# A five-bank attention stage with early operands, and a ring of 16 page pairs for the cached values

## The chip, the cores and the metric

The kernel runs on one core of one Trainium2 chip. The metric is the device time of one execution in microseconds (us). Before the change the median of three runs is 3783.51 us (3782.46 to 3790.58).

## The reference, cut to what matters

The kernel computes one inference step of a decoder layer: input projection, attention beside a state-space branch, output projection, gated feed-forward. Only the attention stage is touched by the change. It has two halves. The prompt half is a strictly causal attention over 2048 positions with 8 heads of 64 channels; the sample half has 8 sequences of one new token each, and each attends to 8192 cached positions, which lie in 64 pages of 128 positions named by a page table.

```
def stick_breaking(q, k, v, bias, q_pos, k_pos):
    z = jnp.einsum('bqhd,bkhd->bhqk', q, k) * (HEAD_DIM ** -0.5)
    z = z + bias[None, :, None, None]
    mask = k_pos[None, :] < q_pos[:, None]
    log_keep = jnp.where(mask, jax.nn.log_sigmoid(-z), 0.0)
    later = lax.cumsum(log_keep, axis=3, reverse=True) - log_keep
    w = jnp.where(mask, jnp.exp(jax.nn.log_sigmoid(z) + later), 0.0)
    return jnp.einsum('bhqk,bkhd->bqhd', w, v)
...
k_past = cache_k[l][page_table].reshape(bs, n_past, N_ATT_HEADS, HEAD_DIM)
v_past = cache_v[l][page_table].reshape(bs, n_past, N_ATT_HEADS, HEAD_DIM)
```

## The kernel before, in words

All of it is in `stage_attention` (from L903). The work runs in eight rounds (`rounds`, L985). Round b works on head b of the prompt and, beside it, on sample sequence b. Round 0 is written out, rounds 1 to 7 are a hardware loop, and a few drain steps follow.

A round has 40 steps, one for each unit (c, j): the 512 queries of chunk c against the 128 keys of block j, chunk 3 first, j falling. A unit goes through a pipeline over the engines. TensorE (PE) writes the logits z by two products (L1373) into PSUM bank s % 4. ScalarE (ACT) makes ln(1 + exp z) in `X` (L1176, L1178). VectorE (DVE) makes the clamped softplus (L1264, one step later). GpSimd (POOL) masks a diagonal block (L1127) and keeps the running sum `S` of the keys already done (L1134, L1140). PE then adds the two triangular or all-ones sums to the same bank (L1383, L1386, L1391, two steps after the logits), ACT takes the exponential into `Wt` (L1184), and PE multiplies with the values (L1406, three steps after, two units at a time). Banks 4 and 5 hold the outputs, bank 6 (`Q_B`) the query of the sample, and bank 7 (`S_B`) the sample's sums.

The sample's work is laid into the same steps. In steps 0 to 31 DVE multiplies one pair of key pages with the query, which it reads from bank 6 (L1295), and reduces the product (L1300). In steps 32 to 37 the sample's softmax-like weights are made (L1309 to L1322 on DVE, L1200 to L1207 on ACT, L1414 and L1415 on PE). In the odd steps up to 31 of the next round PE multiplies two pairs of value pages with these weights (L1343). The last sequence has no next round: its 32 pairs come in a tail after round 7. Key and value pages lie in rings of 8 pairs each (`Kr`, `Vr`).

Before a head's first unit, q and k of the head are split in two parts that TensorE can take at full precision: ACT makes three copies and the bias row (L1163 to L1169), DVE two differences (L1255, L1256). This is done by chunk at steps 0, 1, 5 and 9 of the head's own round (`SPLIT_AT`, L983), from two slots of raw chunks. Each round begins with the spread of the sample's query on DVE (L1248) and its four transposes on PE (L1359); the bias of the head is copied at step 0 (L1269).

Every load is issued by the SyncE queue (SP), in one order, written out in `round_` from L1057. For each n of 0 to 31 it reads two page numbers into registers, waits until DVE has summed key pair n, and issues two DMAs for key pair n + 8 (L1042); then it reads two page numbers, waits until PE has used value pair n of the sequence before, and issues two DMAs for value pair n + 8. Between them lie the raw chunks of q and k (L1021, four DMAs a chunk, four chunks a round), the values of the head (L1030, four a round), and at the round's head three copies of page-table rows (L1060) with a wait for their landing (L1063). A wait in this order holds back all that stands behind it.

Of the kernel before, what the change touches and what calls it, by code (L numbers as in the profile page):

```python
# [15 lines left out]
F32 = mybir.dt.float32  # L16
F32R = mybir.dt.float32r
I32 = mybir.dt.int32
# [4 lines left out]
P = 128  # L23
# [867 lines left out]
KSLOTS, VSLOTS = 8, 8  # L891
# [13 lines left out]
def stage_attention(nc, A, keep):  # L905
# [17 lines left out]
    with ExitStack() as ctx:  # L923
        m = Stage(nc, ctx, "att")
        ident = keep["ident"]
        NX, NW = 4, 4
        row_last, row, row_next = (m.sb(n, [1, NPG], I32) for n in ("row_last", "row", "row_next"))
        table, table_in = m.sb("table", [1, NS, NPG], I32), m.sb("table_in", [1, NS, NPG], I32)
        qf, kf = m.sb("qf", [P, 2, CH]), m.sb("kf", [P, 2, CH])
# [18 lines left out]
        qsT = m.sb("qsT", [P, QT, NS])  # L948
        qrep = m.sb("qrep", [P, QT, P])
        z_s, x_s, w_s = (m.sb(n, [P, H, NPG]) for n in ("z_s", "x_s", "w_s"))  # L950
        R = m.sb("R", [P, H, NPG + 1])
# [4 lines left out]
        Q_B, S_B = 6, 7  # L956
# [6 lines left out]
        q_wide, q_rows = m.sem("q_wide"), m.sem("q_rows")  # L963
        qk_loaded, v_piece = m.sems("qk_loaded", 2), m.sems("v_piece", NCH)
# [14 lines left out]
        LAGS = 5  # L979
        K_END = NKK  # L980
        VG = 2 * PP
        QUAD = P // VG
        SPLIT_AT = {0: 3, 1: 2, 5: 1, 9: 0}  # L983

        def rounds(eng, body):  # L985

            body(0, range(NU), True, False)
# [14 lines left out]
        with nc.Block() as block:  # L1002

            @block.sync
            def _(sp):
                sp.dma_start(table_in[:], A["page_table"][:, :].rearrange("(o b) r -> o b r", o=1)).then_inc(table_loaded, 16)
                sp.dma_start(bias_all[:], A["sb_bias"].to_broadcast([P, H])).then_inc(loaded, 16)
                sp.dma_start(qsT[:], A["qT"].rearrange("(j p) n -> p j n", p=P)[:, :, T:NT]).then_inc(loaded, 16)
# [4 lines left out]
                def load_qk(b, c):  # L1013

                    i = NCH - 1 - c
                    if not (isinstance(b, int) and b == 0 and i < 2):
                        sp.wait_ge(qk_lo, b * 2 * NCH + 2 * (i - 1))
                        sp.nop().then_inc(waited, 1)
                    for x, src in ((qf, "qT"), (kf, "kT")):
                        for half in range(2):  # L1020
                            sp.dma_start(x[half * HD:(half + 1) * HD, i % 2, :], A[src][bass.ds(b * HD, HD), c * CH:(c + 1) * CH]  # L1021
                                         ).then_inc(qk_loaded[i % 2], 16)
# [27 lines left out]
                for c in (3, 2):  # L1050
                    load_qk(0, c)
# [5 lines left out]
                def round_(b, first, last):  # L1057
# [6 lines left out]
                    for n in range(NKK):  # L1064
# [35 lines left out]
            def _(pool):  # L1100
# [5 lines left out]
                pool.memset(R[:], 0.0).then_inc(consts, 1)  # L1106
                pool.wait_ge(consts, 6)
# [38 lines left out]
            def _(act):  # L1146
# [8 lines left out]
                def round_(b, steps, first, rest):  # L1155
                    for s in steps:
                        if s in SPLIT_AT and not rest:
                            c = SPLIT_AT[s]
                            i = NCH - 1 - c
                            cs = slice(c * CH, (c + 1) * CH)  # L1160
                            act.wait_ge(qk_loaded[i % 2], 64 * (b * (NCH // 2) + i // 2 + 1))
                            act.wait_ge(z_ready, b * NU)
                            act.activation(qhh[:, cs], qf[:, i % 2, :], ACT.Copy).then_inc(qk_hi, 1)  # L1163
# [1297 lines left out]
```

## Time and profile before

| what | us |
| --- | --- |
| median of the runs | 3783.51 |
| the profiled execution | 3787.69 |
| its span, first to last instruction | 3786.0 |
| attention, first logits to the store of the samples' output | 739.6 to 1878.2 |
| TensorE busy over the span | 3361.4 (89%) |
| VectorE busy | 2032.3 (54%) |
| ScalarE busy | 1405.9 (37%) |
| GpSimd busy | 640.7 (17%) |

The busy shares are of the whole span; the attention stage is about 30% of it. PE busy is time in which a matmul was under way, and PEclk is the granted clock of TensorE as a share of full speed, 2.4 GHz (0.50 is the lower level, 1.2 GHz). The DMA share is the mean busy share of the 16 DMA engines.

### The profile page before, as it was taken

Reading aid. Unit: us, or ns where it says so; the run is one execution under the profiler, and the core shown is the slowest. Engines: PE = TensorE matmul, PEld = TensorE weight load, DVE = VectorE, ACT = ScalarE, POOL = GpSimd, SP = SyncE. Lnnn points to the kernel's source line nnn. Section 1 sums busy time; section 2 is a strip of 40 time slices with the busy share of each in tenths; the row PEclk is TensorE's granted clock in tenths of the full one; section 3 lists DMA queues with packets and bytes.
Section 4 is the critical chain, followed back from the end, with each engine's and each line's share of the span. In section 5 each row is a group of like instructions: output and inputs, shape, how many; then the busy total and the mean of one; then the engine's idle time right before and its main releaser. Section 6 shows DMA issues by size and latency. Waiting matters only on the chain. (4 is left out here: it accounts for less than half of the span.)

```text
span 3786.0 us, 49489 instructions
## 1 busy us (share of the span) xinstructions
PE 3361.4 (89%) x14901; PEld 2310.0 (61%) x14901; DVE 2032.3 (54%) x2777; ACT 1405.9 (37%) x2206; POOL 640.7 (17%) x902
## 2 busy tenths in 40 slices
PE   4999864589898899889579979999999999999998
PEld 3888742333333333333268857778777877777777
DVE  5010139788788779779245545534553445345542
ACT  4110101256555555555233334423442344223332
POOL 1000047533333333333101100000000000000000
PEclk8999877799999999999789989999999999999999
DMA  4121251377797788779545543343334333433333
GB/s 122 62 72 46 77 77 25 97 238 220 258 310 252 250 280 272 254 259 302 195 139 150 150 115 90 98 146 100 95 103 136 106 95 101 138 121 119 123 113 113
DMA packets 487649, 569.70 MB, mean 150 GB/s; under 512 B 64808, under 2 KB 308616, under 8 KB 485321
## 3 DMA queue, kind: packets, MB, share of 16 engines
q1 hardware_dynamic: 482950, 549.81, 47.7%
q10 hardware_dynamic: 4328, 17.05, 1.2%
q8 instruction: 83, 1.36, 0.2%
q14 instruction: 112, 0.91, 0.1%
q0 software_dynamic: 176, 0.56, 0.0%
HBM read 506.91 MB, written 59.30 MB: 150 GB/s over the span
## 5 line engine op out<-in xcount | busy, mean ns | idle before, releaser
L2088 PE MATMUL ffn_bank<-ffn_xh,ffn_wh 128*128 128x512 f32 x1408 | 557.9, 396 | 18.7 <-DVE ffn_wl L2302 18.3
L2088 PE MATMUL ffn_bank<-ffn_xl,ffn_wh 128*128 128x512 f32 x1408 | 549.5, 390 | 0.0
L2088 PE MATMUL ffn_bank<-ffn_xh,ffn_wl 128*128 128x512 f32 x1408 | 549.0, 390 | 0.0
L1383 PE MATMUL att_bank<-att_X,att_negtri 128*128 128x512 f32 (+3 forms) x640 | 304.0, 557 | 65.1 <-POOL att_X L1127 53.0
L1140 POOL TENSOR_TENSOR att_S<-att_S,att_X 128x512 f32<-128x512 f32 (+3 forms) x256 | 277.7, 1085 | 332.9 <-PE att_bank L1391 183.7
L2088 PEld LDWEIGHTS ffn_bank<-ffn_xh,ffn_wh 128*128 128x128 f32 x1408 | 265.0, 188 | 94.7 <-DVE ffn_wl L2302 31.2
L1300 DVE TENSOR_REDUCE att_z_s<-att_prod 128x16 f32<-128x1024 f32 x256 | 313.0, 1223 | 8.8
L1295 DVE TENSOR_TENSOR att_prod<-att_Kr,att_bank 128x1024 f32<-128x1024 f32 x256 | 310.4, 1213 | 1.7 <-issue 1.7
L2088 PEld LDWEIGHTS ffn_bank<-ffn_xh,ffn_wl 128*128 128x128 f32 x1408 | 265.0, 188 | 56.3
L2088 PEld LDWEIGHTS ffn_bank<-ffn_xl,ffn_wh 128*128 128x128 f32 x1408 | 265.3, 188 | 52.5
L2306 DVE TENSOR_TENSOR ffn_wdl<-ffn_wdf,ffn_wdh 128x1024 fp32r<-128x1024 f32 x88 | 107.5, 1225 | 338.6 <-ACT ffn_wdh L2212 338.5
L1176 ACT ACTIVATE att_X<-att_bank 128x512 f32<-128x512 f32 (+2 forms) x320 | 170.5, 533 | 250.7 <-PE att_bank L1373 250.0
L1391 PE MATMUL att_bank<-att_S,att_negones 128*128 128x512 f32 (+3 forms) x576 | 260.2, 534 | 0.0
L2339 DVE TENSOR_SCALAR ffn_conv<-ffn_gbuf,ffn_prm 128x512 f32<-128x512 f32 x88 | 48.1, 546 | 387.1 <-issue 202.9
L1184 ACT ACTIVATE att_Wt<-att_bank 128x512 f32<-128x512 f32 (+2 forms) x320 | 169.7, 530 | 174.3 <-PE att_bank L1391 171.2
L2190 PE MATMUL ffn_bank<-ffn_wdh,ffn_hh 128*128 128x512 f32 x704 | 221.2, 396 | 11.8 <-DVE ffn_wdl L2306 9.7
L2302 DVE TENSOR_TENSOR ffn_wl<-ffn_stage,ffn_wh 128x1024 fp32r<-128x1024 f32 x176 | 215.0, 1222 | 30.9 <-ACT ffn_wh L2207 29.8
L2212 ACT ACTIVATE ffn_wdh<-ffn_wdf 128x1024 fp32r<-128x1024 f32 x88 | 92.8, 1059 | 349.5 <-PE ffn_bank L2190 320.0
L1264 DVE SCALAR_TENSOR_TENSOR att_X<-att_X,att_bank 128x512 f32<-128x512 f32 (+2 forms) x320 | 191.7, 600 | 54.1 <-ACT att_X L1178 53.2
L2190 PE MATMUL ffn_bank<-ffn_wdl,ffn_hh 128*128 128x512 f32 x704 | 219.5, 393 | 0.0
L2190 PE MATMUL ffn_bank<-ffn_wdh,ffn_hl 128*128 128x512 f32 x704 | 219.4, 393 | 0.0
L2207 ACT ACTIVATE ffn_wh<-ffn_stage 128x1024 fp32r<-128x1024 f32 x176 | 185.8, 1056 | 81.2 <-PE ffn_bank L2088 65.4
(377 smaller groups left out, 5792.4 us busy)
## 6 DMA issues: line engine op xcount, KB each, us to landing
att_Kr<-in_cache_k_dram SPq DMA_DIRECT2D x512, 256.0 KB, 3.7
att_Vr<-in_cache_v_dram SPq DMA_DIRECT2D x512, 256.0 KB, 3.8
ffn_wdf<-in_w_down_dram SPq DMA_DIRECT2D x108, 512.0 KB, 3.6
ffn_stage<-in_w_gate_dram SPq DMA_DIRECT2D x89, 512.0 KB, 3.9
ffn_stage<-in_w_up_dram SPq DMA_DIRECT2D x88, 512.0 KB, 4.6
qku_work<-in_x_prompt_dram SPq DMA_DIRECT2D x16, 512.0 KB
att_qf<-qT_dram SPq DMA_DIRECT2D x64, 128.0 KB, 3.5
att_kf<-kT_dram SPq DMA_DIRECT2D x64, 128.0 KB, 3.6
```

The source lines that it names most:

```text
L1140: pool.tensor_tensor(new[:, r:], old[:, r:], x[:, r:], ALU.add).then_inc(s_part, 1)
L1176: act.activation(x, bank[:, s % 4, cols(s):], ACT.Exp).then_inc(e_ready, 1)
L1184: act.activation(Wt[:, u % NW, cols(u):], bank[:, u % 4, cols(u):], ACT.Exp).then_inc(w_ready, 1)
L1264: stt(x, x, LN_TOP, z, ALU.min, ALU.max).then_inc(sp_ready, 1)
L1295: tt(pr, Kr[:, kk % KSLOTS], bank[:, Q_B, :][:, None, :].to_broadcast([P, PP, AW]), ALU.mult).then_inc(k_used, 1)
L1300: dve.tensor_reduce(z_s[:, :, kk * PP:(kk + 1) * PP].rearrange("p h r -> p r h"), prod[:, kk % 2, :].rearrange("p (k h d) -> p k h d", k=P ...
L1383: last = pe.matmul(bank[:, u % 4, o:], negtri[:], X[:, u % NX, o:], start=False, stop=True, skip_group_check=True)
L1391: last = pe.matmul(bank[:, u % 4, o2:], negones[:], S[:, (u - 1) % 2, o2:], start=False, stop=True, skip_group_check=True)
L2088: mm = pe.matmul(bank[:, first + f % 2, :], w[:, j, k, :], x[:, k, :], start=(k == 0 and n == 0), stop=(k == KD - 1 and n == 2))
L2190: mm = pe.matmul(bank[:, 2 * t + c, :], x[:, f, cols], w[:, sl, c * CH:(c + 1) * CH], start=(f == 0 and n == 0), stop=(f == FT - 1 and n = ...
L2207: act.activation(wh[:, j], wf[:, j], ACT.Copy).then_inc(w_hi[j], 1)
L2302: tt(wl[:, j], wf[:, j], wh[:, j].bitcast(F32), ALU.subtract).then_inc(w_lo[j], 1)
```

## The change: what it does

Five PSUM banks hold logits in place of four, so the second pass over a unit comes three steps after its logits in place of two (`LAG`), and the value product one step later as well. To free a bank, the sample's query is transposed into bank 7 at step 37 of the round before and copied to SBUF (`q_wide`); DVE's product reads it there. The copy takes one ACT instruction; the transposes and the spread move from the round's head into steps 37 and 36. The outputs move to banks 5 and 6.

The raw q and k get four chunk slots. Chunks 3, 2 and 1 of the next head are split at steps 33, 35 and 38 of the round before, chunk 0 at step 3 of its own; the bias is copied at step 28. SP issues all four chunks of head 0 before the first key pages, and later ones at n = 9, 11, 13, 15 of the round before. The head's value pieces 1 and 0 move to n = 1 and 5. The value product of the samples moves from odd to even steps, one step later. Round 7 is written out too.

The ring of value pages has 16 pairs in place of 8; the ring of key pages keeps 8. SP issues value pair n + 16 where it issued pair n + 8, and its count of instructions a round stays.

```diff
-KSLOTS, VSLOTS = 8, 8
+KSLOTS, VSLOTS = 8, 16
...
-        NX, NW = 4, 4
+        NX, NW, NZ = 4, 4, 5
-        qf, kf = m.sb("qf", [P, 2, CH]), m.sb("kf", [P, 2, CH])
+        qf, kf = m.sb("qf", [P, NCH, CH]), m.sb("kf", [P, NCH, CH])
...
+        q_wide = m.sb("q_wide", [P, AW])
-        Q_B, S_B = 6, 7
+        O_B, S_B = NZ, 7
...
-        LAGS = 5
+        LAG = 3
+        LAGS = LAG + 3
+        Q_AT = K_END + 5
-        SPLIT_AT = {0: 3, 1: 2, 5: 1, 9: 0}
+        SPLIT_NEXT = {NKK + 1: 3, NKK + 3: 2, LAST[1] + 3: 1}
+        BIAS_AT = LAST[3] + 13
...
-            with eng.Fori(1, H) as b:
-                body(b, range(NU), False, False)
-            body(H, range(LAGS), False, True)
+            with eng.Fori(1, H - 1) as b:
+                body(b, range(NU), False, False, False)
+            body(H - 1, range(NU), False, True, False)
+            body(H, range(LAGS), False, False, True)
+        def splits(b, s, first, last):
+            now = [(b, 1)] if first and s == 1 else [(b, 0)] if s == 3 else []
+            return now + ([(b + 1, SPLIT_NEXT[s])] if s in SPLIT_NEXT and not last else [])
...
-                    if not (isinstance(b, int) and b == 0 and i < 2):
-                        sp.wait_ge(qk_lo, b * 2 * NCH + 2 * (i - 1))
+                    if not (isinstance(b, int) and b == 0):
+                        sp.wait_ge(qk_lo, (b - 1) * 2 * NCH + 2 * (i + 1))
...
-                for c in (3, 2):
+                for c in reversed(range(NCH)):
                     load_qk(0, c)
...
-                        if n < 2:
-                            load_qk(b, 1 - n)
-                        if n == 2 and not first:
-                            load_v_head(b, 0)
-                        if not last and n in (14, 15):
-                            load_qk(b + 1, 3 if n == 14 else 2)
-                        if not last and n in (20, 30):
+                        if not first and n in (1, 5):
+                            load_v_head(b, 1 if n == 1 else 0)
+                        if not last and n in (9, 11, 13, 15):
+                            load_qk(b + 1, 3 - (n - 9) // 2)
+                        if not last and n in (20, 31):
                             load_v_head(b + 1, 3 if n == 20 else 2)
-                    if not last:
-                        load_v_head(b + 1, 1)
...
+                def copy_queries(b):
+                    act.wait_ge(q_turned, b + 1)
+                    act.wait_ge(k_used, b * NKK)
+                    act.activation(q_wide[:], bank[:, S_B, :], ACT.Copy).then_inc(q_copied, 1)
...
+                        if s == Q_AT + 1 and not last and not rest:
+                            copy_queries(b + 1)
...
-                            tt(pr, Kr[:, kk % KSLOTS], bank[:, Q_B, :][:, None, :].to_broadcast([P, PP, AW]), ALU.mult
+                            tt(pr, Kr[:, kk % KSLOTS], q_wide[:, None, :].to_broadcast([P, PP, AW]), ALU.mult
...
+                        if s == Q_AT - 1 and not last:
+                            spread_queries(b + 1)
...
-                            if not first or s >= 4:
-                                pe.wait_ge(w_ready, units_to(b, s, 4, first))
+                            if not first or s >= NZ:
+                                pe.wait_ge(w_ready, units_to(b, s, NZ, first))
...
-                        r, u = behind(b, s, 2, first, rest)
+                        r, u = behind(b, s, LAG, first, rest)
...
-                        r, u = behind(b, s, 3, first, rest)
+                        r, u = behind(b, s, LAG + 1, first, rest)
...
-                        if s < NKK and not first:
-                            samples_v(b - 1, s)
+                        if 1 <= s <= NKK and not first:
+                            samples_v(b - 1, s - 1)
                         if s == K_END + 1 and not first:
                             finish_sequence(b - 1)
+                        if s == Q_AT and not last_head:
+                            turn_queries(b + 1)
```

## Rows read from the trace of the kernel before

**Rows 1.** Round 2, busy us of PE, PEld, DVE, ACT, POOL; PEclk, DMA share, GB/s:

```profile
1003.80:1139.90 136.10, 123.77 (x488) 52.05 (x488) 111.42 (x134) 77.64 (x143) 48.82 (x63) 0.97 0.84 270
```

**Rows 2.** Waits of PE in round 2 (total us, times, longest):

```profile
PE att_bank L1383 <- POOL att_X L1127: 5.8, 5, 1.9
PE att_bank L1373 <- ACT att_qlb L1169: 3.8, 1, 3.8
PE att_bank L1359 <- DVE att_qrep L1248: 2.6, 1, 2.6
```

**Rows 3.** PE in order of time (start, duration): round starts, a full step, the tail:

```profile
739.62 0.45 PE L1373 MATMUL att_bank<-att_qhh,att_khl 128*128 128x128 f32 x1 [3.05 <-issue]
...
872.59 0.47 PE L1373 MATMUL att_bank<-att_qhh,att_khl 128*128 128x128 f32 x1 [1.90 <-ACT att_qlb L1169]
...
957.02 0.50 PE L1373 MATMUL att_bank<-att_qhh,att_khl 128*128 128x512 f32 x1
...
960.39 0.51 PE L1373 MATMUL att_bank<-att_qhh,att_khl 128*128 128x512 f32 x1
...
1694.93 0.47 PE L1373 MATMUL att_bank<-att_qhh,att_khl 128*128 128x128 f32 x1 [4.00 <-ACT att_qlb L1169]
...
1831.06 1.50 PE L1343 MATMUL att_bank<-att_Vr,att_w_s 128*8 128x512 f32 x12
```

**Rows 4.** Waits of the SP queue in round 2:

```profile
SPq L1042 <- PE att_bank L1343: 3.9, 1, 3.9
SPq L1042 <- DVE att_z_s L1300: 3.2, 1, 3.2
SPq L1028 <- PE att_bank L1406: 2.7, 1, 2.7
SPq L1063 <- DMA att_row_next<-att_table: 1.0, 1, 1.0
```

**Rows 5.** The SP queue in order of time, inside round 1:

```profile
931.87 0.85 SPq L1042 DMA_DIRECT2D att_Kr<-in_cache_k_dram  x2
933.47 0.85 SPq L1042 DMA_DIRECT2D att_Vr<-in_cache_v_dram  x2
934.68 1.16 SPq L1021 DMA_DIRECT2D att_qf<-qT_dram  x2
...
937.88 0.86 SPq L1042 DMA_DIRECT2D att_Kr<-in_cache_k_dram  x2
```

**Rows 6.** DVE in order of time, round 0, one step to the next:

```profile
821.79 1.21 DVE L1295 TENSOR_TENSOR att_prod<-att_Kr,att_bank 128x1024 f32<-128x1024 f32 x1
...
824.77 1.21 DVE L1295 TENSOR_TENSOR att_prod<-att_Kr,att_bank 128x1024 f32<-128x1024 f32 x1
```

**Rows 7.** The SP queue at the start of the stage:

```profile
730.69 1.17 SPq L1021 DMA_DIRECT2D att_qf<-qT_dram  x2
...
736.89 7.46 SPq L1042 DMA_DIRECT2D att_Kr<-in_cache_k_dram  x10
```

**Rows 8.** DVE in round 0, the split of chunk 1:

```profile
763.95 0.68 DVE L1255 TENSOR_TENSOR att_qlb<-att_qf,att_qhh 64x512 fp32r<-64x512 f32 x1 [8.49 <-ACT att_kh L1165]
```

**Rows 9.** What the DMA engines moved in the tail, 1840 to 1870 us:

```profile
DMA packets 5347, 9.76 MB, mean 325 GB/s; under 512 B 593, under 2 KB 593, under 8 KB 5345
```

**Rows 10.** DVE in round 2, step 32, an operation with two SBUF inputs:

```profile
1118.19 0.69 DVE L1309 TENSOR_TENSOR att_z_s<-att_z_s,att_bias_all 128x512 f32<-128x512 f32 x1
```

**Rows 11.** POOL, the mask of a diagonal block, twice in round 2:

```profile
1118.35 0.84 POOL L1127 TENSOR_TENSOR att_X<-att_X,att_keepm 128x128 f32<-128x128 f32 x1 [3.82 <-DVE att_X L1264]
...
1130.79 0.45 POOL L1127 TENSOR_TENSOR att_X<-att_X,att_keepm 128x128 f32<-128x128 f32 x1 [1.52 <-DVE att_X L1264]
```

**Rows 12.** The page: POOL's running sum over the whole kernel (busy us, mean ns):

```profile
L1140 POOL TENSOR_TENSOR att_S<-att_S,att_X 128x512 f32<-128x512 f32 (+3 forms) x256 | 277.7, 1085 | 332.9 <-PE att_bank L1391 183.7
```

**Rows 13.** ACT in round 3, the split of a chunk, first and last instruction:

```profile
1161.87 0.63 ACT L1163 ACTIVATE att_qhh<-att_qf 128x512 fp32r<-128x512 f32 x1 [0.40 <-issue]
...
1163.56 0.72 ACT L1169 ACTIVATE att_qlb<-att_wide,att_bias_now 64x512 fp32r<-64x512 f32 x1
```

More of the change, by code:

```diff
@@ new lines, in copy_queries, with round_ @@
+                def copy_queries(b):
+                    act.wait_ge(q_turned, b + 1)
+                    act.wait_ge(k_used, b * NKK)
+                    act.activation(q_wide[:], bank[:, S_B, :], ACT.Copy).then_inc(q_copied, 1)
+                for c in (3, 2):
+                    split(0, c)
+                copy_queries(0)
+                def round_(b, steps, first, last, rest):
+                    for s in steps:
+                        if not rest:
+                            for at in splits(b, s, first, last):
+                                split(*at)
@@ L1183, in round_ @@
                                 act.wait_ge(av_done, units_to(r, u, NW, first))
-                            act.activation(Wt[:, u % NW, cols(u):], bank[:, u % 4, cols(u):], ACT.Exp).then_inc(w_ready, 1)
-                        r, u = behind(b, s, 4, first, rest)
+                            act.activation(Wt[:, u % NW, cols(u):], bank[:, u % NZ, cols(u):], ACT.Exp).then_inc(w_ready, 1)
+                        r, u = behind(b, s, LAG + 2, first, rest)
                         if u is not None and U[u][1] == 0:
@@ L1190, in round_ @@
                             act.wait_ge(o_copied, r * NCH + chunks - 1)
-                            act.activation(o_odd[:], bank[HD:P, 4 + c % 2, :], ACT.Copy).then_inc(odd_copied, 1)
-                        r, u = behind(b, s, 5, first, rest)
+                            act.activation(o_odd[:], bank[HD:P, O_B + c % 2, :], ACT.Copy).then_inc(odd_copied, 1)
+                        r, u = behind(b, s, LAG + 3, first, rest)
                         if u is not None and U[u][1] == 0:
@@ L1261, in softplus @@
                                 return
[L1262 removed]
+                            x, z = X[:, u % NX, cols(u):], bank[:, u % NZ, cols(u):]
                             dve.wait_ge(l_ready, r * NU + u + 1)
                             stt(x, x, LN_TOP, z, ALU.min, ALU.max).then_inc(sp_ready, 1)
[L1266 to L1269 removed]
+                        if s == BIAS_AT and not rest and not last:
+                            set_bias(b + 1)
                         if s == 0 or not rest:
                             softplus()
[L1272 removed]
+                        r, u = behind(b, s, LAG + 2, first, rest)
                         if u is not None and U[u][1] == 0:
@@ L1337, in samples_v @@
                         pe.wait_ge(w_s_ready, b + 1)
+                        pe.wait_ge(q_copied, min(b + 2, NS) if isinstance(b, int) else b + 2)
                     for i in (n - 1, n):
@@ L1352, in finish_sequence, with turn_queries, round_ @@
                     last.then_inc(col_ready, 1)
-                def round_(b, steps, first, rest):
-                    if not rest:
-                        pe.wait_ge(q_wide, b + 1)
-                        pe.wait_ge(k_used, b * NKK)
-                        for j in range(QT):
-                            last = pe.transpose(bank[:, Q_B, j * P:(j + 1) * P], qrep[:, j, :], ident[:])
-                        last.then_inc(q_rows, 1)
+                def turn_queries(b):
+                    pe.wait_ge(q_spread, b + 1)
+                    pe.wait_ge(logw_s, b)
+                    for j in range(QT):
+                        last = pe.transpose(bank[:, S_B, j * P:(j + 1) * P], qrep[:, j, :], ident[:])
+                    last.then_inc(q_turned, 1)
+                turn_queries(0)
+                def round_(b, steps, first, last_head, rest):
                     for s in steps:
```

103 lines of the change are left out of this document (54 added, 49 removed).

## The prediction

> **What bounds the kernel now.** I read the busy table by stretches first, then PE's waits, then the queue of SP. From the first logits to the store of the samples' output attention lasts 739.6 to 1878.2 us, 1139 of 3786. The eight rounds start 133.0 us apart (round 0) and (1694.93 - 872.59) / 6 = 137.1 us apart on average (rounds 1 to 6); round 7 takes 136.1 and then comes a tail of 47.1 [rows 3]. In round 2 PE is busy 123.8 of 136.1 us, DVE 111.4, ACT 77.6, POOL 48.8 [rows 1]. PE's 12.3 idle us have two places: 6.4 at the round's head (2.6 for the query's spread, 3.8 for the chunk's split and bias), and 5.8 before the second pass over diagonal blocks, which waits for POOL's mask [rows 2]. Everywhere else PE goes without a gap, a full step in 960.39 - 957.02 = 3.37 us [rows 3]. So PE's own work sets the round, and the twelve idle us are what this change can take.
>
> The second thing to see is who stands right behind PE. SP waits in a round only 3.9 + 3.2 + 2.7 us for other engines [rows 4], so its own work is 136.1 - 9.8 = 126.3 us a round (the 1.0 us for the table rows stays with it). Its beat shows the same: a pair of pages every 1.60 us whatever it loads, and 937.88 - 933.47 - 1.60 = 2.8 us more for a chunk of q and k [rows 5]. 64 pairs make 102.4 us, four chunks 11.2, value pieces and table rows the rest. DVE's own beat is 2.98 us a step while keys are multiplied [rows 6], 95.4 us for 32 steps.
>
> **Part 1: the round's head, rounds 1 to 7.** Gone from PE's path are 2.6 + 3.8 us of waits [rows 2]; the four transposes stay, now in step 37. The work is the same number of instructions: the ACT copy of the query is new, one of 0.6 us (the size of the split's own copies [rows 13]), beside PE. A split occupies ACT from 1161.87 to 1164.28, 2.4 us [rows 13], and three of four now fall in steps 33 to 38. I cost this at nothing, since the third step of lag covers it; if that cover is gone it is at most 2.4 us for each of three splits, 7 us a round, and I count 3 us of it as a rival.
>
> **Part 2: the lag of three.** The five waits of 5.8 us on POOL's mask [rows 2] have a longest of 1.9 us; a step is 3.37. One more step of distance covers each. PE's floor is then 136.1 - 12.2 = 123.9 us, a little less (I say 122), since after the idle head PE works some us at the lower clock (PEclk 0.97 over the round [rows 1]).
>
> **Part 3: what is late next.** SP's 126.3 us. The change leaves its instructions in number as they are, and moves a few past one another. Its waits for DVE's first sum and PE's first value pair fall away when it is late itself, and the wait at the round's end for a value piece is moved behind work long done. The key ring keeps 8 pairs, so a late SP reaches DVE some steps later, DVE's product waits in DVE's queue ahead of the softplus, and PE waits for that. The lead of the ring (8 steps of 3 us) holds for a round or so, then the round is SP's. I take 126.3 us a round for rounds 1 to 6: 6 x 126.3 = 757.8 against 822.3, a gain of 64.5. Both ends: 122 (PE's floor) gives 90; DVE's floor is 95.4 for the keys and about 24 for the last eight steps, 120, no bound. Round 7 issues 8 key pairs fewer, so PE's floor holds, 123.9 and 1 more for the longer drain: a gain of 11.2.
>
> The Trainium skill (DMA: Bandwidth & Descriptors, "Issuing engines are not separate DMA queues") says that the sequencer's time to start a DMA is usually small beside the DMA itself. Here the row speaks against it: 1.60 us of queue time for 0.52 MB, and the same bytes take 1.61 us at the tail's 325 GB/s [rows 5, 9]. By the rule SP would bound nothing and rounds would be 122; by the row they are 126.3.
>
> **Part 4: round 0.** It is DVE's: a beat of 2.98 us [rows 6]. Gone are 8.5 us in which DVE waits for the split of chunk 1, whose raw chunk was queued behind key pages [rows 8]. Added: SP issues four chunks before the first key page in place of two; two took 736.89 - 730.69 = 6.2 us [rows 7], so all key products start 6.2 later. The head of round 1 loses 1.9 us of wait in the row at 872.59 [rows 3] and the spread's, 2.5 as in round 2 [rows 2], together 4.4, and PE's logits run one DVE step further ahead of the softplus, 3.0. Against that I set 3 us for the port (part 6). Sum: 8.5 - 6.2 + 4.4 + 3.0 - 3 = 6.7, a gain; bounds 0 and 13.
>
> **Part 5: the ring of 16.** In rounds 1 to 7 nothing waits for value pages (no such row among PE's waits [rows 2]), so the ring brings nothing there, and it costs no instruction. In the tail, 24 pairs are loaded after 1831 us at 325 GB/s [rows 9], 1.61 us a pair, and PE waits for them. With 16 pairs already there 16 remain: a gain of 8 x 1.61 = 12.9. The 4.2 MB move to round 0, whose DVE does not wait for them; if it did, the gain would be gone, so 0 to 13.
>
> **Part 6: the product's operand.** DVE's key product now has both inputs in SBUF. Its own duration I leave at 1.21 us [rows 6]: half as many elements with two SBUF inputs took 0.69 [rows 10], twice that is 1.38, so up to 0.17 a step more, which fits into DVE's spare time. But POOL shows something: the mask that started inside that operation took 0.84 us, the same mask 12 us later 0.45 [rows 10, 11]. So such a DVE operation holds POOL up, by 0.39 us in that row. The reverse, DVE held by POOL, no row shows; it lies between 0 and the longest sum of POOL, 1.28 us (277.7 / 256 gives a mean of 1.09 over all shapes [rows 12]). I take 0.1 us a step, near zero, because DVE has 0.4 us to spare in a full step of PE (3.37 - 2.98), and where DVE is late POOL's sum starts from PE's product, beside DVE's reduction; that is the 3 us of round 0.
>
> The Trainium skill (SBUF — State Buffer, "Who interferes with whom") says that a DVE instruction with two SBUF inputs contends with a GpSimd instruction that reads SBUF, and that whichever starts first makes the other wait until its end. The trace agrees for one direction (0.84 beside 0.45 us). By the rule in full it is the slower rival below.
>
> **The sum.** 64.5 + 11.2 + 6.7 + 12.9 = 95.3. The profiled execution took 3787.7 (span 3786.0), so 3692.4; it lies 4.2 above the median of the runs, 3783.5, so 3688.
>
> **The rivals.**
> - PE stays the bound: rounds of 122. For it: SP's lateness has 8 pairs of lead, and the loads could slide. Against: a lead is spent once, 126.3 comes each round. Six rounds give 26 more, round 7 two: 3660.
> - ACT or DVE is late at the round's end, where three splits, the sample's exponentials and the query's copy now meet: rounds of 129 to 130. For: these eight steps hold 7.2 us of splits that were elsewhere. Against: ACT is busy 77.6 of 136 us [rows 1]. 7 x 3 = 21: 3709.
> - Slower: DVE's product waits for POOL's running sum. It decides from the point where a DVE step with keys exceeds 3.5 us, a wait of 0.52 us a step: then the keys take 112 us and, with 24 for the rest, the round is the old 136. At a wait of half a sum, 0.64 us, the step is 3.62, the round 140, 3 above the old mean: 7 x 3 = 21 slower, round 0 32 x 0.54 = 17 less its 6.7, the tail 12.9 back: 3783.5 + 18 = 3802. At 1.28 us it is near 3960. For: the 0.39 us above. Against: POOL is busy 48.8 of 136 us [rows 1], and a DVE that waits shifts until the two alternate.
> - No change (within 0.2%): some new wait gives all back; I see no such row.
>
> **How the numbers follow.** Forecast 0.50, PE the bound 0.20, crowded end 0.15, slower by the port 0.08, no change 0.03; 0.04 are for things not listed, half on each side. A measurement of this kernel can tell 0.2%, 8 us, from no change. Faster 0.87, same 0.03, slower 0.10. The range runs from 3655, just past PE's floor, to 3730, past the crowded end and a port that costs 6 us a round.
>
> **What would show it.** Right: PE's waits at L1359 and for the bias row gone; no wait for POOL's mask above 0.5 us; starts of rounds 126 us apart from round 2 on; SP's queue without a wait of over 1 us but for table rows; DVE's L1295 waiting for DMA of `att_Kr` late in the key steps; the tail 34 us. Wrong: rounds of 122 with SP waiting for DVE each round (the queue was no bound); L1295 much over 1.21 us, or idle before it released by POOL (the port); PE idle in steps 33 to 39.

## The result: 3731.2 us, and the profile after

| | before | after |
| --- | --- | --- |
| median of four runs each, same chip | 3785.32 (3782.46 to 3790.58) | 3731.23 (3729.65 to 3737.59) |
| ratio | | 0.9859, 95% interval 0.9842 to 0.9876 |
| span of the profiled execution | 3786.0 | 3729.7 |
| round 0 | 133.0 | 125.65 |
| rounds 1 to 6, mean | 137.1 | 132.9 |
| round 7 | 136.1 | 131.3 |
| tail | 47.1 | 34.4 |

The change gains 54 us of the 95 forecast; the forecast was 3688, with a range to 3730, and the median lies 1.2 us beyond it. Of the span's 56.3 us attention accounts for 7.3 + 25.2 + 4.8 + 12.7 = 50.0 by its four stretches (forecast 6.7, 64.5, 11.2, 12.9). The other 6.3 lie before the first logits (1.1) and behind the samples' store (1907.8 before, 1902.6 after). The change has nothing there, and this latter stretch came out between 1901.1 and 1907.6 in the experiments' profiles with no order to it: it is scatter. So the miss is one of rounds 1 to 7: 39.3 us in rounds 1 to 6 and 6.4 in round 7.

PE in order of time in the changed kernel, the starts of rounds 0, 1 and 7 and of the tail, against [rows 3]; then the samples' store on SP's queue:

```profile
738.56 0.48 PE L1415 MATMUL att_bank<-att_qhh,att_khl 128*128 128x128 f32 x1 [1.82 <-DVE att_khl L1283]
...
864.21 0.33 PE L1415 MATMUL att_bank<-att_qhh,att_khl 128*128 128x128 f32 x1
...
1661.37 0.33 PE L1415 MATMUL att_bank<-att_qhh,att_khl 128*128 128x128 f32 x1
...
1792.68 0.63 PE L1382 MATMUL att_bank<-att_Vr,att_w_s 128*8 128x512 f32 x4
```

```profile
1827.11 0.40 SPq L1101 DMA_DIRECT2D attT_dram<-att_att_s  x1
```

A round of the loop in the changed kernel by engines (columns as in [rows 1]), then what PE waited for in it, against [rows 2], and what SP's queue waited for, against [rows 4]:

```profile
1128.75:1262.03 133.28, 124.74 (x490) 54.07 (x488) 114.88 (x133) 77.61 (x145) 62.89 (x65) 0.96 0.86 276
```

```profile
PE att_bank L1390 <- DVE att_own L1261: 3.9, 1, 3.9
PE att_bank L1448 <- ACT att_Wt L1205: 3.2, 2, 2.7
PE att_bank L1425 <- POOL att_X L1135: 1.5, 1, 1.5
```

```profile
SPq L1053 <- DVE att_z_s L1336: 7.4, 1, 7.4
SPq L1074 <- DMA att_row_next<-att_table: 1.0, 1, 1.0
SPq L1053 <- PE att_bank L1382: 0.2, 1, 0.2
```

The waits aimed at are gone: the spread's 2.6 and the bias's 3.8 altogether, POOL's mask from 5.8 to 1.5. Two are new. PE waits 3.9 us at L1390 for DVE's product `att_own` of the finished sequence, and 3.2 us at the round's head for ACT's `Wt`, 2.7 of them in one stop. SP's own work is 133.3 - 7.4 = 125.9 us, as sized (126.3). But it waits for DVE's first key sum of the round, and that comes when the round before has ended: the queue does not bind, it is held to the round's beat.

Both new waits, seen close. DVE in order of time at steps 32 to 34:

```profile
1235.45 0.95 DVE L1345 TENSOR_TENSOR att_z_s<-att_z_s,att_bias_all 128x512 f32<-128x512 f32 x1
1236.44 0.57 DVE L1348 TENSOR_SCALAR att_x_s<-att_z_s 128x512 f32<-128x512 f32 x1
1236.93 1.47 DVE L1282 TENSOR_TENSOR att_qlb<-att_qf,att_qhh 64x512 fp32r<-64x512 f32 x1
1238.44 0.69 DVE L1283 TENSOR_TENSOR att_khl<-att_kf,att_khl 64x512 fp32r<-64x512 f32 x1
1239.16 0.69 DVE L1302 SCALAR_TENSOR_TENSOR att_X<-att_X,att_bank 128x512 f32<-128x512 f32 x1
1239.76 0.69 DVE L1261 TENSOR_TENSOR att_own<-att_bank,att_heads 128x512 f32<-128x512 f32 x1
```

and PE over the same time and at the head of the next round:

```profile
1235.98 0.65 PE L1448 MATMUL att_bank<-att_Wt,att_vh 128*64 128x128 f32 x4
1240.51 1.87 PE L1390 MATMUL att_bank<-att_one,att_own 128*128 128x1 f32 x8 [3.88 <-DVE att_own L1261]
1242.23 0.77 PE L1415 MATMUL att_bank<-att_qhh,att_khl 128*128 128x512 f32 x1
...
1267.37 1.09 PE L1448 MATMUL att_bank<-att_Wt,att_vh 128*64 128x128 f32 x4 [2.43 <-ACT att_Wt L1205]
```

DVE is never idle here. The split of chunk 3 (L1282, L1283) and a softplus stand ahead of the product in its in-order queue, and PE is ready from 1236.6. The stall then costs a second time. Busy time by stretches of 5 us around it:

```profile
1235.00:1240.00 5.00, 1.63 (x10) 0.71 (x8) 4.90 (x7) 4.55 (x9) 2.50 (x3) 1.00 0.98 318
1240.00:1245.00 5.00, 4.50 (x13) 3.27 (x14) 3.37 (x12) 1.23 (x2) 0.00 (x0) 0.51 1.01 353
1245.00:1250.00 5.00, 5.00 (x15) 2.33 (x13) 0.90 (x2) 3.06 (x6) 1.90 (x2) 0.80 0.97 329
```

After 3.9 idle us the granted clock is 0.51, the 1.2 GHz level, for five us, then 0.80 on the way back to 2.4. Against full speed these ten us lose 5 x 0.49 + 5 x 0.20 = 3.4 us of work, an estimate from the two rows, beside the 3.9. ACT at the head of the next round:

```profile
1262.52 0.26 ACT L1205 ACTIVATE att_Wt<-att_bank 128x128 f32<-128x128 f32 x1
1264.85 0.28 ACT L1197 ACTIVATE att_X<-att_bank 128x128 f32<-128x128 f32 x1 [2.07 <-POOL att_S L1148]
1265.16 0.31 ACT L1199 ACTIVATE att_X<-att_X 128x128 f32<-128x128 f32 x1
1266.84 0.38 ACT L1205 ACTIVATE att_Wt<-att_bank 128x256 f32<-128x256 f32 x1 [1.37 <-issue]
```

ACT is idle for 2.07 and 1.37 us, the second time with nothing that the profile shows to wait for. At the head of round 7, which is written out, these gaps are absent, and so they are at the head of round 1, the loop's first pass; PE's wait for `Wt` is 0.5 us in round 1 and 0.7 in round 7. So the loop's turn was suspected.

### The profile page after: what moved, and what is told of

It is laid out like the page before. It is cut to its first block and busy times, and to the rows that moved or that the text cites. A ratio compares the mean times of both kernels' runs of the same rounds, so it can differ in the third digit from the quotient of the medians.

```text
span 3729.7 us, 49239 instructions
## 1 busy us (share of the span) xinstructions
PE 3346.6 (90%) x14901; PEld 2314.4 (62%) x14901; DVE 2056.5 (55%) x2777; ACT 1408.0 (38%) x2214; POOL 759.2 (20%) x903
## 5 line engine op out<-in xcount | busy, mean ns | idle before, releaser
L1148 POOL TENSOR_TENSOR att_S<-att_S,att_X 128x512 f32<-128x512 f32 (+3 forms) x256 | 307.3, 1200 | 342.1 <-PE att_bank L1433 320.0
L1331 DVE TENSOR_TENSOR att_prod<-att_Kr,att_q_wide 128x1024 f32<-128x1024 f32 x256 | 334.0, 1305 | 5.4 <-issue 4.3
```

Source lines behind the costliest of these rows:

```text
L1148: pool.tensor_tensor(new[:, r:], old[:, r:], x[:, r:], ALU.add).then_inc(s_part, 1)
L1331: tt(pr, Kr[:, kk % KSLOTS], q_wide[:, None, :].to_broadcast([P, PP, AW]), ALU.mult).then_inc(k_used, 1)
```

## The experiments

Each is the changed kernel with the edit shown, unless it says otherwise; "round" is the mean of rounds 1 to 6, from PE's starts in the trace. None leaves out any of the work.

| kernel | median us | ratio to before, 95% | round us |
| --- | --- | --- | --- |
| changed kernel | 3731.23 | 0.9859 (0.9842 to 0.9876) | 132.9 |
| e2, own product first | 3710.43 | 0.9801 (0.9778 to 0.9824) | 129.2 |
| e3, split early | 3720.63 | 0.9830 (0.9807 to 0.9852) | 129.9 |
| e5, both | 3709.04 | 0.9790 (0.9769 to 0.9812) | 129.1 |
| e7, before + query in SBUF | 3836.71 | 1.0142 (1.0114 to 1.0169) | 144.0 |
| e1, value ring of 8 | 3748.08 | 0.9892 (0.9869 to 0.9915) | 132.9 |
| e6, before + ring of 16 | 3777.69 | 0.9971 (0.9950 to 0.9992) | 137.4 |
| e9, four banks, query in SBUF | 3762.70 | 0.9921 (0.9898 to 0.9943) | 136.1 |
| e10, four banks, query in PSUM | 3736.16 | 0.9854 (0.9838 to 0.9871) | 134.6 |
| e11, e2 + ring of five X | 3708.31 | 0.9776 (0.9740 to 0.9811) | 128.8 |
| e12, e10 + e2 | 3719.81 | 0.9799 (0.9762 to 0.9837) | 130.5 |
| e13, e2 + merged q/k loads | 3942.73 | 1.0388 (1.0350 to 1.0426) | 159 |
| e14, e11 + merged q/k loads | 3938.96 | 1.0381 (1.0342 to 1.0419) | as e13 |
| e15, e2 + ACT's rounds written out | 3691.92 | 0.9741 (0.9725 to 0.9757) | 127.5 |
| e16, e15 + k chunks issued by ACT | 3685.69 | 0.9724 (0.9707 to 0.9740) | 124.95 |
| e17, e16 + e3 | 3687.28 | 0.9734 (0.9716 to 0.9751) | 125.3 |
| e18, e12 + ACT's rounds written out | 3719.06 | 0.9813 (0.9795 to 0.9830) | 129.5 |

The kernel before was timed anew beside each group of experiments, on three chips, and its median lay between 3785.2 and 3795.7 us. So medians are compared within a group (e2, e3, e5, e7; e1, e6, e9, e10; e11 to e14; e15 to e18), and across groups the ratio is the safer figure: 0.001 of it is 3.8 us. The rounds come from one execution each; that of e10 was 10.7 us above its median and that of e15 5.6, so their rounds read long.

**The order at step 33 (e2, e3, e5).** e2 puts the finished sequence's product ahead of the split on DVE; e3 splits chunk 3 nine steps earlier; e5 has both.

```diff
+                        if s == K_END + 1 and not first and not rest:
+                            finish_sequence(b - 1)
                         if not rest:
                             for at in splits(b, s, first, last):
                                 split(*at)
...
-                        if s == K_END + 1 and not first:
-                            finish_sequence(b - 1)
```

```diff
-        SPLIT_NEXT = {NKK + 1: 3, NKK + 3: 2, LAST[1] + 3: 1}
-        BIAS_AT = LAST[3] + 13
+        SPLIT_NEXT = {LAST[3] + 9: 3, NKK + 3: 2, LAST[1] + 3: 1}
+        BIAS_AT = LAST[3] + 5
```

> The changed kernel with one order changed on VectorE: at step 33 the product for the finished sequence (L1261) stands ahead of the split of the next head's chunk 3, not behind it. Theory A (the end of the round is crowded on in-order queues: PE waits 3.8 to 4.0 us a round for that product, and works on at the low clock after it): the split's 1.47 + 0.69 us and the softplus's 0.6 leave the way of the product, the wait falls to about 1 us, with it some 3 us of slow work if the clock no longer falls: rounds of 133.2 become 127 to 130, the time about 3731 - 7 x 4 = 3703 (3690 to 3715). Theory B (contention of DVE and POOL for SBUF reads sets the round): no change, 3725 to 3735. Theory C (the page queue sets the round, 125.8 us of its own work): no round below 126, so nothing under about 3680; a gain down to there is possible.

> The changed kernel with the next head's chunk 3 split at step 24 in place of 33 (its old operands have been read by step 15), and the bias copied at step 20. Theory A: ACT loses 2.4 us and DVE 2.2 us ahead of the product PE waits for, the wait falls from 3.9 to about 1.5 us, rounds to 128 to 130: 3700 (3690 to 3715). DVE has 0.4 us to spare in a step with full width, so the split at step 24 costs nothing there. Theory B: no change or slower, since two more DVE operations with two SBUF inputs (64x512) run beside POOL: 3725 to 3745. Theory C: no round below 126.

> Both edits together: product ahead, chunk 3 split at step 24. Theory A: the wait for the product is nearly gone (below 0.5 us), but the second wait, 2.4 to 2.7 us for ACT's weights at the next round's first steps, stays: rounds of 126 to 129, 3690 (3675 to 3705), a little under the better of the two alone. Theory C: rounds reach 126 and SP's queue stops waiting for DVE's first sum (now 6 to 7.5 us a round). Theory B: as the changed kernel, 3731.

PE's waits in a round of e2:

```profile
PE att_bank L1448 <- ACT att_Wt L1205: 2.9, 2, 2.4
PE att_bank L1425 <- POOL att_X L1135: 1.5, 1, 1.5
PE att_bank L1456 <- DVE att_R L1354: 0.9, 1, 0.9
PE att_bank L1390 <- DVE att_own L1261: 0.7, 1, 0.7
```

The same round as above by engines, in e2:

```profile
1118.46:1246.18 127.72, 121.69 (x490) 51.93 (x488) 115.13 (x133) 77.21 (x145) 63.02 (x65) 0.99 0.88 285
```

An edit of order alone gives 21 us (22 by the ratios) and takes 3.2 of the 3.9 us of wait; PEclk of that round is 0.99, where it was 0.96. The round is 5.6 us shorter: 3.05 us is less busy PE for the same products (124.74 to 121.69), which is the clock's part, and 2.6 us is less waiting, since 0.9 us for DVE's `att_R` is new. The mean gain is smaller, 3.7 us a round, because PE's wait for `Wt` is 3.5 to 4.5 us in e2's rounds 4 to 6 (2.9 to 3.2 in the changed kernel) and its round 6 took 132.8 at PEclk 0.95. e3 leaves 2.2 of the wait and gives half; both together (e5) give no more than e2 and miss the 3690 expected. The stall at step 33 is shown, and its price with the clock. The wait for `Wt` stays in all three, and SP still waits 1.7 us for DVE in this round of e2.

**The port (e7, e9, e10).** e7 is the kernel before with the query's bank copied to SBUF by ACT, so that the product's operand changes, and one ACT copy a round is new:

```diff
+                                act.activation(q_sb[:], bank[:, Q_B, :], ACT.Copy).then_inc(q_copied, 1)
...
-                            tt(pr, Kr[:, kk % KSLOTS], bank[:, Q_B, :][:, None, :].to_broadcast([P, PP, AW]), ALU.mult
+                            tt(pr, Kr[:, kk % KSLOTS], q_sb[:, None, :].to_broadcast([P, PP, AW]), ALU.mult
```

e9 takes the fifth bank and the third step out of the changed kernel; e10 does so and leaves the query in bank 6:

```diff
-        NX, NW, NZ = 4, 4, 5
+        NX, NW, NZ = 4, 4, 4
-        LAG = 3
+        LAG = 2
```

> The kernel before with one thing of the change: ACT copies the sample's query from bank 6 to SBUF once a round (0.6 us, while it waits for the bias), and DVE's key product reads it there, so it has two SBUF inputs. Theory B (port): POOL's masks of diagonal blocks start behind that product and take 1.2 us more; with a lag of two steps PE waits for them, 14 of 16 a round: its wait of 5.8 us grows to 12 or more, rounds by 6 to 15 us, 3785 becomes 3830 to 3890. Theory A (the port costs little): 3785 to 3800.

> The changed kernel with four logit banks and a lag of two steps (the fifth bank and the third step undone), all else as changed: early operands, query in SBUF. Theory: the third step is what covers the port (POOL's masks of 1.0 to 1.5 us behind DVE's products). Without it PE waits for masks again, more than the 5.8 us a round of before, and its clock falls: rounds of 137 to 142, 3760 to 3800. Rival: the third step brought only the 5.8 us of before: rounds of 136, 3750.

> As the one with four banks and a lag of two, and the sample's query turned into bank 6, which is free again, and read there by DVE's product, so no operation more has two SBUF inputs. Only the early operands and the ring of the change are left. Theory: rounds lose the 6.4 us of the head and keep the 5.8 us for masks, and get the wait for the finished sequence's product (about 4 us and slow work behind it): 132 to 135, 3725 to 3750, within some us of the changed kernel; and well under the one with the query in SBUF, by 7 x 4 us or more. Rival (the port costs nothing at this place): both alike.

POOL's groups (busy us, mean ns, idle before) in a 144 us stretch of e7, sum and mask; then the same two in round 2 of the kernel before:

```profile
L1141 POOL TENSOR_TENSOR att_S<-att_S,att_X 128x512 f32<-128x512 f32 (+3 forms) x33 | 39.4, 1193 | 41.0 <-PE att_bank L1395 36.3 <-DVE att_X L1268 4.7
L1128 POOL TENSOR_TENSOR att_X<-att_X,att_keepm 128x128 f32<-128x128 f32 x16 | 16.0, 1000 | 32.8 <-DVE att_X L1268 32.8
```

```profile
L1140 POOL TENSOR_TENSOR att_S<-att_S,att_X 128x512 f32<-128x512 f32 (+3 forms) x32 | 34.7, 1086 | 40.3 <-PE att_bank L1391 23.2 <-DVE att_X L1264 17.1
L1127 POOL TENSOR_TENSOR att_X<-att_X,att_keepm 128x128 f32<-128x128 f32 x17 | 8.2, 480 | 41.1 <-DVE att_X L1264 41.1
```

A round of e7 by engines, against [rows 1]:

```profile
1308.67:1452.15 143.48, 128.70 (x488) 55.19 (x489) 114.73 (x134) 78.16 (x144) 60.99 (x64) 0.93 0.80 257
```

In the kernel before, that operand costs 51 us: the mask doubles to 1.0 us in the mean, and the round grows by 7. PE's waits for the mask account for 2.6 of these (5.8 to 8.4); the larger part is that PE is busy 4.9 us longer with the same products, at a PEclk of 0.93 where it was 0.97. The copy itself is not what costs: PE's waits at the round's head, for the spread and the bias, are 2.5 and 3.9 us, as before. The third step covers the slower masks in the changed kernel, where they take 1.08 us in the mean and mostly 1.4 beside DVE's products, while PE waits once for 1.5. With both taken out (e10) the time is that of the changed kernel, 0.9854 against 0.9859: the five-bank form, as built, brought nothing beyond what it cost. The port is one of these costs; the last experiment below shows another. With the port cost and without the cover (e9) it is 27 us slower than e10.

**The ring (e1, e6).** One line, `KSLOTS, VSLOTS = 8, 8` in the changed kernel and `8, 16` in the kernel before.

> The changed kernel with 8 pairs of value pages in the ring, as before. If the ring is worth what the tail shows (47.1 us before, 34 after), this is 13 us slower than the changed kernel, 3744, and its rounds are the same 133. If the ring also hides late pages in the rounds, the rounds lengthen and PE shows waits for pages.

> The kernel before with the ring of 16 value pairs alone. Same theory: the tail falls from 47 to 34 us, the rounds stay, 3785 - 13 = 3772. Rival: the 8 more pairs loaded in round 0 delay its key pages, and the gain is smaller.

Rounds are equal with and without. By the ratios to before, e1 gives (0.9892 - 0.9859) x 3785 = 12 us and e6 11 us (3 to 19 by its interval). The traces say it more sharply, and place it in the tail: 47.1 us in e1 against 34.4 in the changed kernel, and 34.4 in e6 against 47.1 before, 12.7 us both times (forecast 12.9).

**What the head of the round waits for (e11, e12, e15).** Two causes were open: the ring of four `X` buffers, or the turn of ACT's hardware loop. e11 adds a fifth `X` to e2 (the room comes from placing `bias_left` in `z_s`):

```diff
-        NX, NW, NZ = 4, 4, 5
+        NX, NW, NZ = 5, 4, 5
```

e15 writes ACT's rounds out and leaves all other engines in the loop:

```diff
-                rounds(act, round_)
+                round_(0, range(NU), True, False, False)
+                for b in range(1, H):
+                    round_(b, range(NU), False, b == H - 1, False)
+                round_(H, range(LAGS), False, False, True)
```

> The changed kernel with the finished sequence's product ahead of the split, and a ring of five softplus tiles X in place of four (a small bias tile shares the place of another, to fit). With the product ahead PE still waits 2.9 to 4.1 us a round at the next head's first steps for ACT's weights, and ACT waits there 4 to 6 us for POOL's sums before it may write X again. Theory A (ring of X is the cause): both waits fall below 1 us, rounds of 128 to 129 become 125.5 to 127, 3710 becomes 3690 (3680 to 3700). Rival: the wait moves to POOL's sums themselves, no change. Theory C (page queue, 126 us of own work) holds rounds at 126 whatever else is freed.

> Four banks, lag of two, query read from bank 6, early operands, ring of 16, and the finished sequence's product ahead of the split. If that order costs the same here as in the changed kernel (21 us), 3736 becomes 3715; the fifth bank with its lag is then worth the same few us with and without it. If the wait there is hidden behind POOL's masks (lag of two), the gain is smaller, 3725.

> The kernel with the product ahead of the split, and ACT's rounds 1 to 6 written out in place of a loop (the other engines keep theirs). At the head of a looped round ACT stands 3.2 + 1.5 us without work of its own, at the head of round 7, which is written out, not at all, and PE waits 2.9 to 4.1 us a round for ACT's weights there, 0.7 in round 7. Theory A2 (ACT's turn of the loop is the second wait): PE's wait falls to 0.7, rounds of 128 to 129 become 125 to 126, 3710 becomes 3693 (3685 to 3700). If it is the place in the pipeline and not the turn: no change. Theory C: SP's waits for DVE's first sum (1.7 to 3 us) go to zero and rounds stop at 126.

ACT at the same point of the same round in e11, then in e15:

```profile
1250.53 0.28 ACT L1198 ACTIVATE att_X<-att_bank 128x128 f32<-128x128 f32 x1 [3.52 <-issue]
1250.84 0.31 ACT L1200 ACTIVATE att_X<-att_X 128x128 f32<-128x128 f32 x1
1252.51 0.38 ACT L1206 ACTIVATE att_Wt<-att_bank 128x256 f32<-128x256 f32 x1 [1.35 <-issue]
```

```profile
1246.01 0.27 ACT L1197 ACTIVATE att_X<-att_bank 128x128 f32<-128x128 f32 x1
1246.31 0.31 ACT L1199 ACTIVATE att_X<-att_X 128x128 f32<-128x128 f32 x1
1246.78 0.38 ACT L1205 ACTIVATE att_Wt<-att_bank 128x256 f32<-128x256 f32 x1 [0.16 <-PE att_bank L1436]
```

A fifth `X` changes little but the label of the gap, which is now "issue": rounds of 128.8 against 129.2, and PE's wait for `Wt` in this round 4.3 us against 4.1 in e2. The theory of the ring fell. Written out, both gaps are gone, PE's wait for `Wt` is 0.5 us, and the time falls by another 18 us to 3691.9 (23 by the ratios), where the forecast had 3688. SP's waits in a round of e15, the only line that is left:

```profile
SPq L1074 <- DMA att_row_next<-att_table: 1.5, 1, 1.5
```

From round 2 on SP no longer waits for any engine, and DVE's product waits for pages (0.6 us in this round). Rounds 3 to 5 take 125.8 to 126.3 us; the mean of 127.5 has rounds 2 and 6 in it, 130.1 and 129.4, in which PE waited 3.4 us for `att_own`; what delayed it there is open. The rounds of 126 are the state which Part 3 of the prediction described.

**Is the queue then the bound (e13, e14, e16, e17)?** Two ways to take work from it. e13 and e14 load both halves of a q or k chunk by one DMA with a broadcast source; e16 lets ACT's queue issue the raw k chunks at steps 9 to 15.

```diff
-                        for half in range(2):
-                            sp.dma_start(x[half * HD:(half + 1) * HD, i, :], A[src][bass.ds(b * HD, HD), c * CH:(c + 1) * CH]
-                                         ).then_inc(qk_loaded[i], 16)
+                        sp.dma_start(x[:, i, :], A[src][bass.ds(b * HD, HD), c * CH:(c + 1) * CH][None].to_broadcast([2, HD, CH])
+                                     ).then_inc(qk_loaded[i], 16)
```

```diff
+                        if s in (9, 11, 13, 15) and not last and not rest:
...
+                            for half in range(2):
+                                act.dma_start(kf[half * HD:(half + 1) * HD, i, :], A["kT"][(b + 1) * HD:(b + 2) * HD, c * CH:(c + 1) * CH]
+                                              ).then_inc(qk_loaded[i], 16)
```

> As the one with the product ahead of the split (3710), and the raw q and k chunks loaded by two DMAs a chunk in place of four (one DMA fills both halves of the partitions): 8 DMAs fewer a round, about 5 of SP's 126 us. Theory C: SP waits only 1.7 to 3 us a round for DVE there, so the queue is nearly the bound: its lateness goes, rounds lose 1 to 3 us, 3700. Theory A alone: SP waits 5 us longer, the rounds stay, 3705 to 3713.

> Product ahead, ring of five X, merged loads. Theory C: where the ring of five alone stops at rounds of 126, this one goes on to 123 to 125, 3675 to 3685, at least 7 us under it. If SP bounds nothing, it equals the ring of five alone within noise.

> As the one with ACT written out, and the raw k chunks of the next head issued by ACT at steps 9 to 15, so SP's queue has 8 DMAs a round less, some 5 of its 126 us. Theory C: if rounds of ACT written out are held by the queue, these are 2 to 4 us shorter, about 123, 3675. If the queue holds nothing: the same, 3693, with SP waiting 5 us longer a round.

> As the last, and chunk 3 split at step 24. The product that PE waits for was then 0.8 us later than without the early split (1.5 beside 0.7), since DVE had less to do but later; so within 5 us of the last, either side. It is the version with every stall found so far taken out.

The SP queue of e13 in order of time, then DVE's longest waits over one round of it:

```profile
1452.31 0.60 SPq L1031 DMA_DIRECT2D att_qf<-qT_dram  x1
1453.03 5.49 SPq L1031 DMA_DIRECT2D att_kf<-kT_dram  x1
1459.78 3.91 SPq L1052 DMA_DIRECT2D att_Kr<-in_cache_k_dram  x1
```

```profile
DVE att_prod L1332 <- DMA att_Kr<-in_cache_k_dram: 30.8, 3, 11.8
```

What the DMA engines did while that queue was held, in e13 (the last two columns are their mean busy share and GB/s):

```profile
1453.10:1454.50 1.40, 1.40 (x10) 0.16 (x9) 1.37 (x2) 0.52 (x1) 0.32 (x1) 1.00 1.07 294
1456.00:1458.50 2.50, 2.50 (x10) 0.86 (x9) 2.46 (x4) 0.92 (x2) 0.43 (x1) 1.00 0.13 50
```

The merged loads failed at what they were for. Once the pages ahead of them have landed, the mean busy share of the 16 DMA engines is 0.13, what two of them fully busy would give, at 50 GB/s; it stays at 0.13 to 0.18 until 1464.5, and 0.5 MB at 50 GB/s is 10 us. In that time the second merged load of the pair, or the key DMA behind it, holds the queue for 2.8 to 5.5 us, where a merged load takes 0.6 when it is not held; in the round from 1238.7 us the second load was held in three of four pairs, for 4.5 to 5.5 us. So one DMA with a doubled source is no cheap form of two. By that e13 became a test of the opposite sign: a queue that is late costs the whole kernel, by the path queue, DVE's product, softplus, PE (159 us a round).

e16 takes the eight DMAs from SP in a way that works, but for less than expected (3675): 3685.7 us, 6.2 below e15, with no run of one inside the range of the other. Its rounds are 124.4 to 125.3, under the queue's 126. In round 3 of it SP waits for DVE again (3.7 us) and PEclk is 1.00 with four us of waits of PE, so PE is the bound. The bytes a round are those of e15, and they move at 294 to 296 GB/s where e15 had 290: it was the queue and not the DMA engines that held e15, a rival worth naming, because SP's beat of 1.60 us a pair is also what 325 GB/s gives. e17 adds nothing to e16. The changed kernel is 45.5 us above e16 by the medians, 51 by the ratios.

**The fifth bank, with and without ACT's turn (e12, e18).** e12 is e10 with the product ahead of the split, and e18 is e12 with ACT's rounds written out, that is, e15 with the four banks of e10.

> Four banks, lag of two, query in PSUM, product ahead, ACT written out: what the fifth bank is worth once the two waits at the round's end are gone. With the fifth bank the time is expected at 3693; here PE still waits some 4 to 6 us a round for masks: rounds of 130, 3715. If it lies within 5 us of the five-bank form, the fifth bank only pays for the port contention it brings.

PE's waits in a round of e12, then in one of e18:

```profile
PE att_bank L1420 <- POOL att_X L1135: 8.7, 6, 2.4
PE att_bank L1443 <- ACT att_Wt L1203: 0.6, 1, 0.6
```

```profile
PE att_bank L1423 <- POOL att_X L1135: 8.2, 5, 2.4
```

In the four-bank form the masks hold PE, and the turn costs next to nothing. ACT stands for 2.02 + 1.40 us at the round's head in e12 too, but PE waits 0.5 to 1.3 us for `Wt` in its rounds 2 to 6, not 2.9 to 4.5, and writing ACT's rounds out changes the time by 0.7 us (3719.8 to 3719.1; the ratios 0.9799 and 0.9813 do not tell them apart). With five banks and three steps the same edit gives 18. So the turn is a cost that the form with five banks brings into view, beside that of the port. While the turn stays, the form is worth little (0.9801 in e2, 0.9799 in e12); once it is gone, 3719.1 - 3691.9 = 27 us. Why three steps of lag expose the turn and two do not was not tried.

## Why the prediction was wrong

- **Part 1, the failing step.** "... three of four now fall in steps 33 to 38. I cost this at nothing, since the third step of lag covers it". The lag covers the way from logits to softplus. It does not cover an instruction for which PE waits in the same step: the finished sequence's product, behind the split on DVE. That is 3.9 us of wait a round and about 3 us of work at the low clock, and e2 takes back 21 us. The rival of a crowded end named the place (129 to 130 a round); it was the right mechanism, priced at 3 us a round where e2 gives 3.7 in the mean, and it missed the second stall beside it.
- **Not in the prediction at all:** ACT's loop turn, 3.4 us of idle ACT and 2.9 to 3.2 of PE's in rounds 2 to 6. e15 takes back 18 us. It is not the removal of the waits for the spread and the bias that let it appear: e9, e10 and e12 have them removed too, with a lag of two, and PE waits there for `Wt` at most 1.3 us a round. It came with the five banks and the third step. Writing out the loop of the kernel before was not tried.
- **Part 3, the size right and the role wrong.** SP's own work is 125.9 us (forecast 126.3). It binds only when both stalls are out (e15: 125.8 to 126.3 in rounds 3 to 5, 127.5 in the mean). Of the 39.3 us missing in rounds 1 to 6 (6 x 6.6), e2 and e15 return 6 x 5.4 = 32. For round 7 the forecast took PE's floor from round 2, 123.9 us and 1 for the drain. But PE is busy 127.2 us in round 7 (128.2 before), and waits 4.2 more, 1.6 of them for `att_own`. So it gained 4.8 where 11.2 were forecast.
- **Part 2.** Right: PE's waits for the mask went from 5.8 to 1.5, although the port made the masks longer, 0.48 to 1.08 us in the mean. That the third step would have to cover masks of 1.4 us was not foreseen; e9 and e10 show that it did.
- **Part 4.** Forecast 6.7, measured 7.3, in part by luck. DVE's wait of 8.5 us for chunk 1 is gone, as forecast, and the first key product comes 5.06 us later (745.50 against 740.44; forecast 6.2). But DVE's beat is unchanged at 2.99, so the 3 us set for the port do not show. The two terms for the next round's head, 7.4 together, must then have come to about 3.9 (7.3 - 8.5 + 5.1); which of them was too large is open. (For the spread the sum has 2.5 us where [rows 2] have 2.6.)
- **Part 5.** Forecast 12.9, measured 12.7, and again 12.7 in the tails of e1 and e6.
- **Part 6.** DVE's product takes 1305 ns in the mean, 0.09 a step more (forecast 0.1). The price lay on POOL's side, whose busy time in a round rose from 48.8 to 62.9 us, and was hidden. The forecast had no term for that, and e7 shows the 51 us which it costs when uncovered, most of it by the clock. The slower rival had named the wrong victim: not DVE behind the sum, but PE behind the mask.
- **The range** ended at 3730 because the rivals were taken one at a time. A crowded end (3709) with a second, unnamed stall of about its size is what happened, and that lies at the range's edge.

## What to carry to other kernels

When waits are cleared from the bound engine's path, list for every step that receives moved work each instruction on the same in-order queue that another engine awaits in that same step; lag hides only the chain which it lengthens. A deeper pipeline can expose a wait that the shallow one hid (here a loop's turn on ACT), so test an edit in both forms before calling it worthless. Price a stall of some us on TensorE twice, for the idle time and for the low clock after it; here that was 3.2 and 3.05 us in one round. An engine's own work is a bound only after every stall that is longer than its slack is gone.

## What the hardware showed that was not expected

- **The port works both ways, by who starts first.** DVE's product, then POOL's sum, in a round of the changed kernel:

```profile
1176.03 1.60 DVE L1331 TENSOR_TENSOR att_prod<-att_Kr,att_q_wide 128x1024 f32<-128x1024 f32 x1
```

```profile
1175.27 1.28 POOL L1148 TENSOR_TENSOR att_S<-att_S,att_X 128x512 f32<-128x512 f32 x1 [2.08 <-PE att_bank L1433]
```

  POOL began first, and the product takes 1.60 us where it has 1.22 alone. In round 0 DVE begins first, and the sum takes up to 2.12 us, where its median is 1.28, while the product stays at 1.22:

```profile
786.85 1.22 DVE L1331 TENSOR_TENSOR att_prod<-att_Kr,att_q_wide 128x1024 f32<-128x1024 f32 x1
```

```profile
787.09 2.11 POOL L1148 TENSOR_TENSOR att_S<-att_S,att_X 128x512 f32<-128x512 f32 x1 [0.87 <-DVE att_X L1302]
```

  The Trainium skill (SBUF — State Buffer, "Who interferes with whom") says that the port pair which the two engines share is an exclusive lock, and that issue order decides who blocks. The traces agree in both directions: the sum ends 1.13 us after the product's end, the product 1.08 us after the sum's, each nearly its own length.
- **A loop's turn on ACT** stopped it for 2.07 + 1.37 us here, 3.52 + 1.35 in e11 and 2.02 + 1.40 in e12; written out it is 0 + 0.16 (e15). What it cost the kernel was 18 us in one form and under 1 in another.
- **A DMA with a doubled source** (an outer dimension of two and a step of zero) left the 16 DMA engines at a mean busy share of 0.13 and 50 GB/s, where the pages just before ran at 0.95 and 318 GB/s (1440 to 1443 us of e13), and its queue was held for 4.25 and 5.49 us in the two pairs seen there.
- **The granted clock** was 0.51 in the five us after 3.9 idle ones, in a stretch where PE was then busy 4.50 of 5.00.
